# First norm of a two-block network: the input loaded from two queues, root and gain in one operation, 13 warming products

## The chip, the cores and the metric

The kernel runs on one core of a Trainium2 chip. The time is the device time of one execution in microseconds (us); for the kernel before, the median of three runs. Engines: PE is TensorE (matrix products), PEld its weight loads, DVE is VectorE, ACT is ScalarE, POOL is GpSimd, SP is SyncE, which here only issues DMAs. The names with q (SPq, ACTq) are the issue of DMAs on that engine; q1 is SP's DMA queue and q10 ScalarE's.

## The reference

256 positions of width 1024 go through two blocks: the first has two layers (sparse attention and a state-space mixer, each followed by a gated feed-forward), the second one (a gated delta rule with attention to a memory, then a feed-forward). All is float32. The change touches only the first norm and how its input comes in:

```python
def rms_norm(x, gain):
    xf = x.astype(jnp.float32)
    y = xf * lax.rsqrt(jnp.mean(xf * xf, axis=-1, keepdims=True) + RMS_EPS)
    return (y * gain.astype(jnp.float32)).astype(x.dtype)

def first_block(x, norm_gains, nsa_w_in, ...):
    h = x
    for i in range(DEPTH):
        gains = norm_gains[i]
        hn = rms_norm(h, gains[0])
        m = nsa_mixer(hn, nsa_w_in[slot], ...)   # i = 0; its first step is hn @ w_in
...
```

## The kernel before

Each engine has a program of its own, written in order; semaphores join them. Every weight matrix is cut into blocks of 1 MB (128 partitions x 2048 float32), which `sp_load` (L490) fetches into three buffers `raw`, one SP DMA each, in the order of a plan. ScalarE copies a block in two pieces into a high part `whi` (`act_high`, L513), VectorE subtracts to get the low part `wlo` (`dve_low`, L521). The activations are split in the same way into a high and a low `xT`, and TensorE makes every product of three (`pe_three`, L537: low by high, high by low, high by high).

At the start there are two tiles of 128 rows, t = 0 and 1, each in two halves of 512 columns, n = 0 and 1:

- SP issues the four halves of the input into `h` (L2826), then three weight blocks (L496) and small tables. ScalarE issues the identity matrix (L2846, shown as masks<-in_masks) and the gain row, broadcast to 128 partitions, into `grow2` (L617, shown as grow<-in_rows), and loads its activation table.
- ScalarE squares each half with a running sum (`act_norm_sums`, L679). VectorE adds the two sums of a tile (L684), GpSimd takes the power -1/2 (L667).
- Meanwhile VectorE multiplies each half by the gain (`dve_norm_gain`, L697); when the root is there it scales the result in place (`dve_norm_scale`, L704). The halves are then ready in `xs` or `xs1`.
- TensorE starts as soon as the identity has landed with 16 products of it with itself, whose result nobody reads (L3005, the warming products). Then it transposes the halves, four 128x128 pieces each (L725), makes eight more such products (L3009), and begins the first projection with `pe_first` (L1009: first the pieces k 0 to 3 of the high parts, then 4 to 7; then L1015 and L1016 with the low parts).
- ScalarE copies the transposed halves into the high `xT` (L734), tile 0, then a piece of the first weight block (L519), then tile 1, then the next piece; VectorE makes the low `xT` (L741) and low weights (L527) in the same order.

From there on the order around the change is written out by hand; no scheduler decides it. The functions that the change touches follow, with what calls them.

Of the kernel before, what the change touches and what calls it, by code (L numbers as in the profile page):

```python
# [259 lines left out]
def build(nc, wall, x_d, mem_d, cols_d, rows_d, masks_d, neg_d, out_d):  # L260
# [6 lines left out]
    MUL, ADD, SUB = ALU.mult, ALU.add, ALU.subtract  # L267
# [12 lines left out]
    with root:  # L280
# [11 lines left out]
        def up(sem, *event, by=1):  # L292
            return counts[0].up(sem, *event, by=by)

        def at(sem, *event):
            return counts[0].at(sem, *event)
# [4 lines left out]
        def sb(shape, dt=f32, st=root, name="t"):  # L301
            names[0] += 1
            return st.enter_context(nc.sbuf_tensor(f"{name}{names[0]}", shape, dt))
# [16 lines left out]
        h = sb([128, 2, 1024], name="h")  # L320
        xT = [sb([128, 8, 256], f32r, name="xT") for _ in range(2)]
        ss = sb([128, 8], name="ss")
        rr = sb([128, 4], name="rr")
        sqj = sb([128, 1024], name="sqj")
        xs = sb([128, 1024], name="xs")
        grow2 = sb([128, 1024], name="grow2")
# [140 lines left out]
        def rowsrc(name, a=0, n=None):  # L467
            o, w = _ROWS[name]
            n = w if n is None else n
            return rows_d[:, o + a:o + a + n].to_broadcast([128, n])  # L470
# [145 lines left out]
        def act_gain(e, i, name):  # L616
            e.dma_start(gains[i][:, :], rowsrc(name)).then_inc(*up(f"gain{i}", name, by=16))  # L617

        def xs_of(k, t):

            return xs1 if t and k != 4 else xs

        def halves(v):
            return [v[:, 512 * n:512 * n + 512] for n in range(2)]
# [66 lines left out]
        def dve_norm_gain(e, k, t, n, src, gain, ready, turned=None):  # L691

            e.wait_ge(*at("gain1", gain))
            e.wait_ge(*at(*ready[n]))
            if turned:
                e.wait_ge(*at("pe.norm", *turned))
            e.tensor_tensor(halves(xs_of(k, t))[n], halves(src)[n], grow2[:, 512 * n:512 * n + 512], MUL).then_inc(  # L697
                *up("dve.norm", "y", k, t, n))

        def dve_norm_scale(e, k, t):  # L700
            e.wait_ge(*at("pool.norm", "sum", k, t))
            for n, v in enumerate(halves(xs_of(k, t))):
                e.wait_ge(*at("dve.norm", "y", k, t, n))
                e.tensor_scalar(v, v, rr[:, 2 * t + 1:2 * t + 2], None, MUL).then_inc(*up("dve.norm", "xs", k, t, n))  # L704
# [22 lines left out]

        def four(b):
            return b[:, :].rearrange("p (a n) -> p a n", a=4)

        def act_norm_high(e, k, t, ns=range(2)):
            for n in ns:
# [2088 lines left out]


        def sync(e):
            for t in range(2):
                for n in range(2):
                    e.dma_start(h[:, t, 512 * n:512 * n + 512], x_d[128 * t:128 * t + 128, 512 * n:512 * n + 512]).then_inc(  # L2826
                        *up(f"h{t}{n}", by=16))
            for i in range(NRAW):
                sp_load(e, i)
            e.dma_start(cols[:, :], cols_d).then_inc(*up("cols", by=16))  # L2830
            e.dma_start(negf[:, :], neg_d).then_inc(*up("negf", by=16))
            e.dma_start(masks[:, 128:_MASKS], masks_d[:, 128:_MASKS]).then_inc(*up("masks", by=16))
            for o, name in ((0, "dtb"), (32, "alog"), (64, "gdtb"), (72, "galog")):
                e.dma_start(srow[:, o:o + _ROWS[name][1]], rowsrc(name)).then_inc(*up("srow", name, by=16))
            for i in range(NRAW, NCH):
                sp_load(e, i)
            for t in range(2):
                for n in range(2):
                    o = 512 * n
                    e.wait_ge(*at("dve.norm", "h", 5, t, n))  # L2840
                    e.dma_start(out_d[128 * t:128 * t + 128, o:o + 512], h[:, t, o:o + 512]).then_inc(*up("out", by=16))
            e.wait_ge(*last("out"))

        def scalar(e):
            split = Split(lambda p: act_high(e, p), ENDS)
            e.dma_start(ident, masks_d[:, 0:128]).then_inc(*up("ident", by=16))  # L2846
            act_gain(e, 1, "g_nsa")
            e.wait_ge(*at("pool.const", "nhalf"))
            e.activation(rr[:, 0:1], nhalf[:, :], ACTF.Square).then_inc(*up("act.const", "table"))
            for t in range(2):  # L2850
                act_norm_sums(e, 0, t, h[:, t, :], [(f"h{t}{n}",) for n in range(2)])
            act_norm_high(e, 0, 0)
            split.one()
            act_norm_high(e, 0, 1)
            split.to(2)
            act_nsa_in(e, split)
            e.wait_ge(*at("dve.const", "gon"))
            e.wait_ge(*at("srow", "galog"))
            e.wait_ge(*at("dve.norm", "y", 0, 1, 1))
            act_gain(e, 1, "g_ffn0")  # L2860
            walk(NSA_ORDER["act"], {"s": scoring(nothing, lambda n: act_exp(e, n)),
                             "t": turning(nothing, lambda n: act_turned(e, n)),
                             "v": valuing(nothing, lambda t: act_close(e, t), four_steps()),
                             "b": act_nsa_cmp(e), "c": act_nsa_side(e)}, split)
            split.to(C_OUT + 4)
            act_add_norm(e, 0, 1, (C_OUT + 3,))
            split.to(C_OUT + 5)
            act_norm_sums(e, 1, 1, h[:, 1, :], hready(0, 1))
            act_norm_high(e, 1, 1)

            e.wait_ge(*at("dve.norm", "mp", 0, 1, 0))
            act_gain(e, 0, "p_ffn0")
            e.wait_ge(*at("dve.norm", "y", 1, 1, 1))
            act_gain(e, 1, "g_ssd")
            act_ffn(e, split, 0)
            act_boundary(e, split, 1, 2, ffn_done(0), C_S + 2, 2)

            act_ssd_first(e, split)
            e.wait_ge(*at("dve.norm", "mp", 1, 1, 0))
            act_gain(e, 0, "p_ssd")  # L2880
            e.wait_ge(*at("dve.norm", "y", 2, 1, 1))
            act_gain(e, 1, "g_ffn1")
            walk(SSD_ORDER["act"], {"a": scans(lambda g, t: act_seg(e, g, t), lambda g: act_ssd_scan(e, g)),
                             "b": projs(lambda g: act_ssd_proj(e, g), no_steps)}, split)
            split.to(C_SO + 8)
            act_boundary(e, split, 2, 3, [(C_SO + 7, "first"), (C_SO + 7,)], C_SO + 7 + AHEAD, 1)

            e.wait_ge(*at("dve.norm", "mp", 2, 1, 0))
            act_gain(e, 0, "p_ffn1")
            e.wait_ge(*at("dve.norm", "y", 3, 1, 1))  # L2890
            act_gain(e, 1, "g_mem")
            e.wait_ge(*at("pe.norm", 3, 1, 1))
            e.dma_start(memx[:, :, :], mem_d.rearrange("(t p) d -> p t d", p=128)).then_inc(*up("mem", by=16))
            act_ffn(e, split, 1, lambda g: act_mem_rows(e, g))
            act_gdn_in(e, split, ffn_done(1))
            e.wait_ge(*at("dve.norm", "mp", 3, 1, 0))
            act_gain(e, 0, "p_gdn")
            e.wait_ge(*at("dve.norm", "y", 5, 1, 1))
            act_gain(e, 1, "g_ffn2")
            walk(GDN_ORDER["act"], {**{s: chains(i, lambda hp: act_chain(e, hp)) for i, s in enumerate("ab")},  # L2900
                             "c": fill(lambda j: act_gproj(e, j), no_steps),
                             "p": first_pair(lambda j: act_gproj(e, j)),
                             "m": mem_attention(lambda n: act_mem_exp(e, n), lambda n: n % 2 or act_mem_turned(e, n), nothing, lambda: act_mem_end(e))}, split)
            act_boundary(e, split, 4, 6, [(C_GO + 5, "first"), (C_GO + 5,)], C_GO + 5 + AHEAD, 1)

            e.wait_ge(*at("dve.norm", "mp", 4, 1, 0))
            act_gain(e, 0, "p_ffn2")
            act_ffn(e, split, 2)
            for t in range(2):
                act_add_norm(e, 5, t, ffn_done(2)[t])  # L2910

        def vector(e):
            split = Split(lambda p: dve_low(e, p), ENDS)
            e.wait_ge(*at("act.const", "table"))
            for t in range(2):
                for n in range(2):
                    dve_norm_gain(e, 0, t, n, h[:, t, :], "g_nsa", [(f"h{t}{n}",) for n in range(2)])
                dve_norm_sums(e, 0, t)
            for t in range(2):
                dve_norm_scale(e, 0, t)  # L2920
            dve_norm_low(e, 0, 0)
            split.one()
            dve_norm_low(e, 0, 1)
# [76 lines left out]
        def tensor(e):  # L3000
            split = Split(lambda p: None, ENDS)
            e.wait_ge(*at("ident"))

            for _ in range(16):
                e.matmul(banks[0][:, 0:128], ident, ident, start=True, stop=True)  # L3005
            for t in range(2):
                pe_norm_turn(e, 0, t)
# [119 lines left out]
```

## Time and profile before

| | |
|---|---|
| median of 3 runs | 1204.3 us (1203.85 to 1208.6) |
| profiled execution | 1204.32 us |
| its span | 1202.5 us |
| TensorE busy | 1176.9 us, 98% of the span |
| VectorE, ScalarE, GpSimd busy | 70%, 54%, 13% |
| granted TensorE clock | 1.00 in the mean |
| input half, gain row, weight block | 256, 512, 1024 KB per DMA |

The profiled execution agrees with the median. Times in the rows below are counted from the start of the span. A matrix product of two float32 operands of 128x128 (L3005, L3009) is shown as two records of a matmul and two of a weight load, so 16 products are x32. A record's duration is longer than the step from one to the next, since they are pipelined. What stands in square brackets is the idle time before an instruction on its engine, and what ended it; an instruction without a bracket followed the one before at once.

### The profile page before, as it was taken

The numbers are of one execution on the slowest core, as the hardware profiler recorded it, in microseconds if no ns is written. First come the engines' busy times: TensorE is split into PE (matmuls) and PEld (weight loads), VectorE is DVE, ScalarE is ACT, GpSimd is POOL, SyncE is SP. The second block draws the span as 40 slices with busy tenths as digits, with TensorE's granted clock in tenths as the row PEclk, the third lists the DMA queues.
The fourth block names the chain that finished last, engine by engine and source line by source line (L and its number), as shares of the span: only waits on it lengthen the run. The fifth ranks groups of instructions, "written<-read, shape, count | busy, mean of one in ns | idle before, by whom it ended". The sixth has DMA issues, their size and how long they took to land.

```text
span 1202.5 us, 23183 instructions
## 1 busy us (share of the span) xinstructions
PE 1176.9 (98%) x9852; PEld 1076.7 (90%) x9852; DVE 847.2 (70%) x1299; ACT 651.3 (54%) x1171; POOL 151.4 (13%) x143
## 2 busy tenths in 40 slices
PE   8999999999999999999999999999999999999998
PEld 8897789999889898978999988999989878999986
DVE  6677777888557988886788874857577776655542
ACT  4657556666446665644666653665435534644431
POOL 1320000000002332101000000103443311000000
PEclk9999999999999999999999999999999999999999
DMA  8842225565625443353755564442222322755540
GB/s 308 268 141 89 98 101 207 192 210 194 231 106 176 151 182 141 114 184 105 259 196 181 206 245 158 178 176 106 107 107 71 120 93 92 277 196 190 184 167 35
DMA packets 31622, 196.67 MB, mean 164 GB/s; under 512 B 4000, under 2 KB 5664, under 8 KB 9376
## 3 DMA queue, kind: packets, MB, share of 16 engines
q1 hardware_dynamic: 27504, 185.17, 43.1%
q10 hardware_dynamic: 4016, 10.03, 2.6%
q8 instruction: 77, 1.26, 0.5%
q14 instruction: 25, 0.20, 0.0%
HBM read 193.09 MB, written 1.05 MB: 161 GB/s over the span
## 4 chain that ended last, share of the span: by engine, by line
PE 88%; DVE 5%; ACT 3%; issue 2%; POOL 1%; DMA 0%; DVEq 0%; POOLq 0%; ACTq 0%
PE bank L538 24%; PE bank L540 24%; PE bank L539 24%; DVE wlo L527 2%; PE bank L1894 1%; PE bank L1132 1%; PE bank L1189 1%; PE bank L1216 1%; ACT whi L519 1%; PE bank L725 1%; PE bank L2538 1%; PE bank L3005 1%; PE bank L2481 1%; POOL rr L667 0%; PE bank L2525 0%
## 5 line engine op out<-in xcount | busy, mean ns | idle before, releaser
L527 DVE TENSOR_TENSOR wlo<-raw,whi 128x1024 fp32r<-128x1024 f32 x322 | 389.0, 1245 | 87.9 <-ACT whi L519 87.3
L538 PE MATMUL bank<-xT,wlo 128*128 128x256 f32 x1488 | 418.6, 281 | 4.2 <-DVE wlo L527 2.1
L539 PE MATMUL bank<-xT,whi 128*128 128x256 f32 x1488 | 413.1, 278 | 0.0
L540 PE MATMUL bank<-xT,whi 128*128 128x256 f32 x1488 | 413.1, 278 | 0.0
L519 ACT ACTIVATE whi<-raw 128x1024 fp32r<-128x1024 f32 (+1 forms) x349 | 349.2, 1048 | 115.9 <-PE bank L540 86.7
L538 PEld LDWEIGHTS bank<-xT,wlo 128*128 128x128 f32 x1488 | 279.5, 188 | 7.9 <-DVE xc L1601 2.8
L539 PEld LDWEIGHTS bank<-xT,whi 128*128 128x128 f32 x1488 | 279.6, 188 | 0.6 <-issue 0.5
L540 PEld LDWEIGHTS bank<-xT,whi 128*128 128x128 f32 x1488 | 279.4, 188 | 0.0
L667 POOL TENSOR_TENSOR rr<-rr,nhalf 128x1 f32<-128x1 f32 x34 | 24.7, 729 | 710.0 <-DVE rr L655 522.4
L538 PE MATMUL bank<-whi,gT 128*128 128x512 f32 x264 | 104.6, 396 | 0.0
L540 PE MATMUL bank<-whi,gT 128*128 128x512 f32 x264 | 104.4, 395 | 0.0
L539 PE MATMUL bank<-wlo,gT 128*128 128x512 f32 x264 | 104.3, 395 | 0.0
L538 PE MATMUL bank<-whi,xT 128*128 128x256 f32 (+1 forms) x320 | 95.9, 300 | 2.5 <-DVE xT L741 2.5
L539 PE MATMUL bank<-wlo,xT 128*128 128x256 f32 (+1 forms) x320 | 93.0, 291 | 0.0
L540 PE MATMUL bank<-whi,xT 128*128 128x256 f32 (+1 forms) x320 | 93.0, 291 | 0.0
L535 POOL TENSOR_TENSOR wlo<-raw,whi 128x1024 fp32r<-128x1024 f32 x24 | 61.4, 2561 | 118.9 <-ACT whi L519 110.2
L538 PEld LDWEIGHTS bank<-whi,xT 128*128 128x128 f32 x320 | 60.4, 189 | 7.4 <-DVE xT L741 2.8
L539 PEld LDWEIGHTS bank<-wlo,xT 128*128 128x128 f32 x320 | 60.4, 189 | 1.8 <-issue 0.5
L540 PEld LDWEIGHTS bank<-whi,xT 128*128 128x128 f32 x320 | 60.2, 188 | 1.5
L540 PEld LDWEIGHTS bank<-whi,gT 128*128 128x128 f32 x264 | 49.6, 188 | 12.0
L539 PEld LDWEIGHTS bank<-wlo,gT 128*128 128x128 f32 x264 | 49.6, 188 | 11.7
L538 PEld LDWEIGHTS bank<-whi,gT 128*128 128x128 f32 x264 | 49.6, 188 | 11.7
(390 smaller groups left out, 1766.5 us busy)
## 6 DMA issues: line engine op xcount, KB each, us to landing
raw<-in_wall SPq DMA_DIRECT2D x173, 1024.0 KB, 4.8
grow<-in_rows ACTq DMA_DIRECT2D x13, 512.0 KB, 5.3
h<-in_x SPq DMA_DIRECT2D x4, 256.0 KB, 5.3
dsk<-in_rows ACTq DMA_DIRECT2D x4, 256.0 KB, 3.4
memx<-in_mem ACTq DMA_DIRECT2D x1, 1024.0 KB, 10.5
out<-h SPq DMA_DIRECT2D x4, 256.0 KB, 2.0
masks<-in_masks SPq DMA_DIRECT2D x1, 580.0 KB, 13.3
D<-Tx ACTq DMA_DIRECT2D x4, 128.0 KB, 5.8
```

The lines of the kernel that those rows point to most:

```text
L519: e.activation(high, src, ACTF.Copy).then_inc(*up("act.high", p))
L527: e.tensor_tensor(low, src, high, SUB).then_inc(*up("dve.low", p))
L535: e.tensor_tensor(low, src, high, SUB).then_inc(*up("pool.low", p))
L538: e.matmul(out, a[1], b[0], start=start, stop=False)
L539: e.matmul(out, a[0], b[1], start=False, stop=False)
L540: return e.matmul(out, a[0], b[0], start=False, stop=stop)
L667: return e.tensor_tensor(v, v, nhalf[:, :].to_broadcast([128, n]), ALU.pow)
L725: r = e.transpose(tl(turn_bank(k, t, n), j), tl(xs_of(k, t), c), ident)
L1132: r = e.matmul(tl(wbank(2 * m + p), i * (t + 1) + kb), qT[rows, 4 * (g // 2) + h0 + i, 128 * t:128 * t + 128], tl(kz[br][rows, g // 2, :], ...
L1189: r = e.transpose(tl(wbank(n), kb * k + i), tl(aP[place(n)], i * (W // 128) + kb), ident)
L1216: r = e.matmul(banks[6 + g // 2][64 * p:64 * p + 64, 128 * h0:128 * h0 + 128 * k], vv[br][:, kb, 64 * (g + p):64 * (g + p) + 64], aPT[(2 * ...
L1894: r = e.matmul(banks[4][:, 64 * i:64 * i + 64], E[:, i, :], xdt[:, 64 * i:64 * i + 64], start=True, stop=True)
```

## The change

Three things are changed, all in the first microseconds. The halves n = 1 of both input tiles are issued by ScalarE, between the identity and the gain row; SP issues only the halves n = 0 and then goes on to the weights. VectorE no longer multiplies by the gain while it waits for the root: it adds the sums of both tiles, and then one operation per half, `scalar_tensor_tensor`, computes h times root times gain. TensorE makes 13 instead of 16 warming products. ScalarE's wait before it loads the next gain row (L2859) now names the new operation.

```diff
+        def load_h(e, n):
+
+            for t in range(2):
+                e.dma_start(h[:, t, 512 * n:512 * n + 512], x_d[128 * t:128 * t + 128, 512 * n:512 * n + 512]).then_inc(
+                    *up(f"h{t}{n}", by=16))
+
+        def dve_norm_first(e, t):
+
+            e.wait_ge(*at("pool.norm", "sum", 0, t))
+            e.wait_ge(*at("gain1", "g_nsa"))
+            for n in range(2):
+                e.wait_ge(*at(f"h{t}{n}"))
+                e.scalar_tensor_tensor(halves(xs_of(0, t))[n], h[:, t, 512 * n:512 * n + 512], rr[:, 2 * t + 1:2 * t + 2],
+                                       grow2[:, 512 * n:512 * n + 512], MUL, MUL).then_inc(*up("dve.norm", "xs", 0, t, n))
...
         def sync(e):
-            for t in range(2):
-                for n in range(2):
-                    e.dma_start(h[:, t, 512 * n:512 * n + 512], x_d[128 * t:128 * t + 128, 512 * n:512 * n + 512]).then_inc(
-                        *up(f"h{t}{n}", by=16))
+            load_h(e, 0)
...
             e.dma_start(ident, masks_d[:, 0:128]).then_inc(*up("ident", by=16))
+            load_h(e, 1)
             act_gain(e, 1, "g_nsa")
...
-            e.wait_ge(*at("dve.norm", "y", 0, 1, 1))
+            e.wait_ge(*at("dve.norm", "xs", 0, 1, 1))
             act_gain(e, 1, "g_ffn0")
...
             for t in range(2):
-                for n in range(2):
-                    dve_norm_gain(e, 0, t, n, h[:, t, :], "g_nsa", [(f"h{t}{n}",) for n in range(2)])
                 dve_norm_sums(e, 0, t)
             for t in range(2):
-                dve_norm_scale(e, 0, t)
+                dve_norm_first(e, t)
...
-            for _ in range(16):
+            for _ in range(13):
                 e.matmul(banks[0][:, 0:128], ident, ident, start=True, stop=True)
```

How the instructions stand on VectorE from its first one on, before (-) and in the changed kernel (+); `ss` holds the sums, `rr` the roots:

```order
-L697 TENSOR_TENSOR xs<-h,grow 128x512 x2
-L684 TENSOR_SCALAR rr<-ss 128x1
-L697 TENSOR_TENSOR xs<-h,grow 128x512 x2
-L684 TENSOR_SCALAR rr<-ss 128x1
-L704 TENSOR_SCALAR xs<-xs,rr 128x512 x4
-L741 TENSOR_TENSOR xT<-bank,xT 128x4x128 x2
-L527 TENSOR_TENSOR wlo<-raw,whi 128x1024
-L741 TENSOR_TENSOR xT<-bank,xT 128x4x128 x2
+L3072 UNCONDITIONAL_BRANCH
+L684 TENSOR_SCALAR rr<-ss 128x1 x2
+L743 SCALAR_TENSOR_TENSOR xs<-h,rr,grow 128x512 x4
+L756 TENSOR_TENSOR xT<-bank,xT 128x4x128 x2
+L527 TENSOR_TENSOR wlo<-raw,whi 128x1024
+L756 TENSOR_TENSOR xT<-bank,xT 128x4x128 x2
```

Eight operations over the halves have become four, and both sums stand ahead of all of them.

On ScalarE, from its first instruction on (the line numbers move because functions were added):

```order
-L3057 UNCONDITIONAL_BRANCH
-L2846 DMA masks<-in_masks 128x128
+L3068 UNCONDITIONAL_BRANCH
+L2858 DMA masks<-in_masks 128x128
+L734 DMA h<-in_x 128x512 x2
 L617 DMA grow<-in_rows 128x1024
-L2849 ACT_TABLE_LOAD
-L2849 ACTIVATE rr<-nhalf 128x1
+L2862 ACT_TABLE_LOAD
+L2862 ACTIVATE rr<-nhalf 128x1
 L679 ACTIVATE sqj,ss<-h 128x512 x4
```

Two issues of input halves now stand between the identity's and the gain row's, and ahead of the table load.

## Rows read from the trace of the kernel before

**Rows 1.** The page: TensorE's busy time; the chain that ended last, by engine.

```profile
PE 1176.9 (98%) x9852; PEld 1076.7 (90%) x9852; DVE 847.2 (70%) x1299; ACT 651.3 (54%) x1171; POOL 151.4 (13%) x143
...
PE 88%; DVE 5%; ACT 3%; issue 2%; POOL 1%; DMA 0%; DVEq 0%; POOLq 0%; ACTq 0%
```

**Rows 2.** Chain of waits from 0 us: start, duration, what, x records.

```profile
4.22 6.76 PE bank L3005 x32
10.98 1.75 PE bank L725 x16
12.73 1.79 PE bank L3009 x16
```

**Rows 3.** Timeline: start, duration (us), engine, line, operation, [idle before, releaser].

```profile
0.72 1.81 SPq L2826 DMA_DIRECT2D h<-in_x  x4
...
1.17 0.45 ACTq L617 DMA_DIRECT2D grow<-in_rows  x1
...
2.58 1.60 SPq L496 DMA_DIRECT2D raw<-in_wall  x3
...
4.02 0.63 ACT L679 ACTIVATE sqj<-h 128x512 f32<-128x512 f32 x1 [0.87 <-DMA h<-in_x]
...
5.92 0.63 ACT L679 ACTIVATE sqj<-h 128x512 f32<-128x512 f32 x1 [1.18 <-DMA h<-in_x]
...
6.57 1.29 DVE L697 TENSOR_TENSOR xs<-h,grow 128x512 f32<-128x512 f32 x2 [6.57 <-DMA grow<-in_rows]
7.65 0.63 ACT L679 ACTIVATE sqj<-h 128x512 f32<-128x512 f32 x1 [1.00 <-DMA h<-in_x]
...
8.14 0.86 POOL L667 TENSOR_TENSOR rr<-rr,nhalf 128x1 f32<-128x1 f32 x1 [7.32 <-DVE rr L684]
...
8.27 0.62 ACT L679 ACTIVATE sqj<-h 128x512 f32<-128x512 f32 x1
...
9.23 1.82 DVE L704 TENSOR_SCALAR xs<-xs,rr 128x512 f32<-128x512 f32 x4
...
10.82 1.91 PE L725 MATMUL bank<-masks,xs 128*128 128x128 f32 x16
11.45 1.09 ACT L734 ACTIVATE xT<-bank 128x512 fp32r<-128x512 f32 x2 [2.47 <-PE bank L725]
...
12.56 1.95 PE L3009 MATMUL bank<-masks 128*128 128x128 f32 x16
...
14.27 2.40 PE L1009 MATMUL bank<-xT,whi 128*128 128x256 f32 x16
...
15.45 1.01 PEld L1009 LDWEIGHTS bank<-xT,whi 128*128 128x128 f32 x8 [0.20 <-ACT whi L519]
```

**Rows 4.** Line L3005, 4 to 10 and 10 to 13 us: duration ns min/median/max.

```profile
L3005 PE MATMUL bank<-masks x27: 420/422/582, 4.2 to 9.9; 128*128 128x128 f32 x27
...
L3005 PE MATMUL bank<-masks x7: 275/291/422, 9.7 to 10.7; 128*128 128x128 f32 x7
```

**Rows 5.** Timeline of VectorE at 157 us: two three-operand operations.

```profile
157.31 1.41 DVE L664 SCALAR_TENSOR_TENSOR h<-xs,rr,h 128x512 f32<-128x512 f32 x2 [0.73 <-POOL rr L667]
```

**Rows 6.** DMA: queues' packets, MB, share (4.75, 54.75 us); busy by stretch, DMA share, GB/s.

```profile
q10 hardware_dynamic: 16, 0.07, 97.5%
q1 hardware_dynamic: 10, 0.01, 7.9%
...
q1 hardware_dynamic: 9, 0.07, 69.6%
q10 hardware_dynamic: 9, 0.04, 36.0%
...
6.00:7.00 1.00, 1.00 (x7) 1.00 (x6) 0.43 (x1) 0.64 (x2) 0.00 (x0) 1.00 0.87 291
8.00:9.00 1.00, 1.00 (x7) 1.00 (x6) 1.00 (x2) 0.98 (x4) 0.86 (x1) 1.00 1.00 426
```

## What the change is predicted to do

> **What bounds the kernel now.** I read the page's busy shares first [rows 1]: TensorE is busy in 98% of a span of 1202.5 us, and the chain that ended last runs through it for 88%. So a change at the start counts by as much as it moves the moment at which TensorE's dense work begins, no more; after that TensorE is the bound. Second, the chain of waits over the first 16 us [rows 2]: warming products (L3005), transposes (L725), eight more products (L3009). On the chain nothing waits for VectorE or a DMA there: the warming products end after the normalised rows are ready, and they, not the norm, hold the first transpose. Third, the timeline of that stretch [rows 3]: the gain row is used from 6.57, ScalarE's four squares start at 4.02, 5.92, 7.65 (each released by its half of the input) and 8.27 (back to back, so the last half was there), VectorE's last four scalings run from 9.23 to 11.05, TensorE's first transpose starts at 10.82, its first real product (L1009) at 14.27, and its second half waits 0.20 for ScalarE at 15.45. Counting that wait, the dense work starts effectively at 14.27 + 0.20 = 14.47. That is the number to beat.
>
> **Fewer warming products.** 16 products show as 32 records. The granted clock reads 1.00 in all slices, yet 27 records that touch the time before 10.0 last 422 ns and those after it 291 and less [rows 4]: the products go at the pace of the lower level (1.2 GHz) first and of 2.4 GHz from about 10.1, after 5.9 us of unbroken products. From 4.22 to the last slow one at 9.9 there are 26 steps, 0.218 us each. 13 products are 26 records, so the next instruction can start at 4.22 + 26 x 0.218 = 9.9. Against 10.82 this frees 0.9 us, if the rows are ready by then.
>
> **Root and weights in one operation.** VectorE loses four products with the gain and four scalings, which took 1.82 in a row [rows 3], and gets four operations of three operands. Two of that kind take 1.41 together elsewhere, 0.75 for one and 0.66 from start to start [rows 5]. So if the first can start at S, the halves are ready at S + 0.75, S + 1.41, S + 2.07, S + 2.73. The products with the gain used to lie beside the wait for the squares and cost nothing; now the gain row stands directly ahead of the first half. That is the new wait: behind it on VectorE stand all four halves, and TensorE, ScalarE's copies and all else wait for these.
>
> **The loads.** Two halves of the input move from SP's queue to ScalarE's, ahead of the gain. The gain was issued at 1.17; two issues of about 0.45 go before it [rows 3], so now at about 2.07. SP gets to the three weight blocks (1 MB each) two issues earlier, at about 1.65 instead of 2.58: so the first block is now issued before the gain, where it stood 1.4 us behind. The table load and the small square on ScalarE end 0.9 us later, at about 4.05; the squares began at 4.02, so that costs nothing.
> - The input. Without the gain's 0.52 MB ahead of it, at 0.29 MB per us (the rate at 6 to 7 us, rows 6), the last half lands 1.8 us before 8.2, at 6.4. Then the squares run until about 7.2, and with 0.2 on VectorE and 0.86 on GpSimd (the row at 8.14) the roots are done at about 6.9 and 8.3. They are not late.
> - The gain. Where a gain row and a weight block were both under way, nine packets of the one went beside nine of the other in a quarter of a microsecond, 4 KB against 8 KB [rows 6]: they take turns packet by packet, so the block takes two bytes for one of the gain's. Also, before, the input's queue moved next to nothing at 4.75 to 5.0 while the gain filled its own [rows 6], so what is issued earlier holds up what is issued later. Bounds for the landing: with the gain alone behind the input, 0.52 MB at 0.43 MB per us (8 to 9 us, rows 6) is 1.2, so 6.4 + 1.2 = 7.6. With two weight blocks alongside (packets paired off from the start, as the eight packets per DMA engine of each issue would be) it is 2.62 MB, 6.2 us, 12.6. I take one block: 1.57 MB, 3.7 us, so S = 10.1. It is the case nearest to the row at 54.75, where a gain issued shortly behind one block shared the way with that block.
>
> **The sum.** With S = 10.1 the last half is ready at 12.83. Four transposes follow (about 0.11 from start to start, from the 16 between 10.82 and 12.56) with some 0.06 for the signal, then the eight products take 12.56 to 14.27, 1.71. First real product: 12.83 + 0.06 + 0.44 + 1.71 = 15.04. ScalarE is not later than that: its copy of the first turned half came 0.63 after the first transpose, and its last piece before the second half of L1009 4.0 after this (11.45 to 15.45); from a first transpose at 10.91 this gives 15.54, while TensorE asks for it at 15.04 + 0.94. So the 0.20 wait goes, and the start moves from 14.47 to 15.04: 0.6 us later. The profiled execution took 1204.32 for a span of 1202.5, and the median is 1204.3, so the two need no correction: 1204.3 + 0.6 = **1204.9 us**. All in all no change that can be measured: 0.5% (6 us) is what a measurement of this kernel tells from none, and its three runs lie 4.8 apart.
>
> What is costed at nothing: the reload of the weight buffers, which waits for VectorE, shifts with the start, but is needed by TensorE only three blocks (5.6 us of products each) later; the first block arrived before ScalarE came to it at 12.42 without a wait.
>
> On the loads the Trainium skill (DMA: Bandwidth & Descriptors, section "Issuing engines are not separate DMA queues") says that DMAs issued by different engines run on the same 16 DMA engines and that spreading them saves only issue time. The packets taking turns in rows 6 agree with that. It speaks against the first part of the change: by it the input gets ahead only because the gain falls back.
>
> **The rivals.**
> 1. *The gain lands early* (before 9.3). For it: a DMA that is issued earlier holds up later ones, and the gain is issued before two of the three blocks. At S = 7.6 the rows are ready in time, and TensorE goes straight from the warming products at 9.9 into 16 transposes (1.75, plus 0.1 for the slow ones before 10.1), the eight products from 11.75, the first real one at 13.46. ScalarE's chain then gives 9.9 + 0.1 + 0.63 + 4.0 = 14.65 for the second half, against 15.45: 0.8 faster, 1203.5.
> 2. *The input's halves land no earlier than before*, a mechanism of the shared engines: the last at 8.2, its root at 10.14 as before, the gain meanwhile by 9.0. Then the third half starts at 10.2, the last is ready at 11.6, the first real product at 11.6 + 2.2 = 13.8: about 0.6 faster, 1203.7. Against it: the gain's 0.52 MB are no longer between them. The page named above would have it so for the same bytes.
> 3. *The gain lands late*, paired with the second block, at 12.6: every microsecond behind 9.5 is one lost, 17.54 instead of 14.47: 3.1 slower, 1207.4.
> 4. *The clock*, the clearly slower case. The warming products now end at 9.9, and TensorE stands still until S + 0.75, 10.85 by my sum and 13.35 at the late bound. Before, the pace rose at 10.1 after 5.9 us without a gap. If the gap makes it rise only after another 5.9 us, half of that, 2.95, is lost: 1207.9, and with the gain at its late bound 1204.3 + 3.1 + 2.95 = 1210.4. It decides as soon as the gain lands after 9.15. Against it: only 0.2 us of the 5.9 are missing when the products end. The Trainium skill (TensorE: Matmul & The Clock Gate, Part 1) says that the number of slow products at a kernel's start varies between runs of the same kernel; one trace cannot show that.
>
> **How the numbers follow.** Forecast (gain lands between 9.3 and 11.3): 0.42. Rival 1: 0.25. Rival 2: 0.10. Rival 3: 0.15. Rival 4: 0.08. The cases reach from 1203.5 to 1207.9 without the last sum; with 2 us below, because 1200 us of later waits never fall out exactly alike, and 0.6 above, the range is 1201.5 to 1208.5. Faster by over 0.5% (under 1198.3) would need something that no row shows: 0.03. Slower by over 0.5% (over 1210.3) is the far end of rival 4, and what I don't see: 0.06. The same: 0.91.
>
> **What would show it.** Right: the changed timeline has the four squares nearly back to back from about 4 us, VectorE's first three-operand operation released by the gain's DMA near 10, four of them 0.66 apart, TensorE idle before L725, and L1009 (now L1024) first at about 15.0. Rival 1 is seen by L725 following the warming products without a gap, rival 2 by squares released at the old times, rival 3 by a gain at 11.5 or later, rival 4 by transposes and the eight products at 422 ns a record. Wrong as a whole would be a total away from 1204 by more than the first 16 us moved: then something later than the start was touched.

## The result and the profile after

| | before | changed |
|---|---|---|
| median, 20 runs each | 1204.59 us (1203.67 to 1211.88) | 1210.05 us (1208.68 to 1218.07) |
| profiled execution, span | 1204.32, 1202.5 us | 1214.50, 1212.7 us |
| granted TensorE clock, mean | 1.00 | 0.997 |

The changed kernel is slower by 0.45% (ratio 1.0045, 95% interval 1.003 to 1.006), 5.5 us between the medians. The forecast was 1204.9 with a range up to 1208.5: the time lies outside.

First the timeline of the start in the changed kernel (start, duration, engine, line, operation, idle before and releaser). It answers to [rows 3].

```profile
0.72 0.86 SPq L734 DMA_DIRECT2D h<-in_x  x2
...
1.17 0.93 ACTq L734 DMA_DIRECT2D h<-in_x  x2
1.63 1.58 SPq L496 DMA_DIRECT2D raw<-in_wall  x3
2.13 0.45 ACTq L617 DMA_DIRECT2D grow<-in_rows  x1
...
4.02 0.61 ACT L679 ACTIVATE sqj<-h 128x512 f32<-128x512 f32 x1
...
4.12 5.80 PE L3016 MATMUL bank<-masks 128*128 128x128 f32 x26 [4.12 <-DMA masks<-in_masks]
...
5.72 0.63 ACT L679 ACTIVATE sqj<-h 128x512 f32<-128x512 f32 x1 [1.00 <-DMA h<-in_x]
...
9.54 0.63 ACT L679 ACTIVATE sqj<-h 128x512 f32<-128x512 f32 x1 [2.35 <-DMA h<-in_x]
...
13.43 2.74 DVE L743 SCALAR_TENSOR_TENSOR xs<-h,rr,grow 128x512 f32<-128x512 f32 x4 [2.92 <-DMA grow<-in_rows]
...
14.24 3.67 PE L725 MATMUL bank<-masks,xs 128*128 128x128 f32 x16 [4.32 <-DVE xs L743]
...
17.70 3.01 PE L3020 MATMUL bank<-masks 128*128 128x128 f32 x16
...
20.47 2.13 PE L1024 MATMUL bank<-xT,whi 128*128 128x256 f32 x16
```

The warming products end at 9.9, the time that was summed. The last half of the input is squared at 9.54 (before 8.27), the gain row releases VectorE at 13.43 (before 6.57), and TensorE stands still for 4.32 ahead of its first transpose. The first real product starts at 20.47 where it started at 14.27.

TensorE by stretch (busy, records, granted clock, DMA share, GB/s) shows what the pause does:

```profile
12.00:13.00 1.00, 0.00 (x0) 1.00 1.04 434
13.00:14.00 1.00, 0.00 (x0) 0.54 1.02 434
...
16.00:17.00 1.00, 1.00 (x6) 0.50 1.05 430
...
19.00:20.00 1.00, 1.00 (x7) 0.54 0.00 0
20.00:21.00 1.00, 1.00 (x11) 1.00 0.00 0
```

The granted clock falls from 1.00 to 0.50 (2.4 to 1.2 GHz) between 13 and 14 us, after TensorE has done nothing from 9.9 on, and comes back between 19 and 20. All 16 transposes and most of the eight products behind them run at the lower level: the transposes' 421 ns a record (273 before) stand in the next row, which has shortest, median and longest record of line L725.

```profile
L725 PE MATMUL bank<-masks,xs x16: 421/421/473, 14.2 to 17.5; 128*128 128x128 f32 x16
```

Last the DMA queues at 9.5 to 10 us (q1 is SP's, q10 ScalarE's; packets, MB, share of the engines), to be laid beside [rows 6]:

```profile
q1 hardware_dynamic: 19, 0.16, 73.4%
q10 hardware_dynamic: 19, 0.08, 37.8%
```

19 packets against 19. SP's are a weight block's of 8 KB, ScalarE's the gain row's of 4 KB. So the gain gets a third of the bytes.

**Where the rest of the profile differs.** Matching VectorE's operations of both traces, everything from 54 us to 1040 us is later by 5.6 to 6.4 us (5.95 at 54 us, 6.35 at 1040); hardly anything further is lost in 980 us. In the profiled execution the last feed-forward layer then adds 4. That has nothing to do with the change, as the last section shows, and is why the two spans lie 10.2 apart and the medians 5.5.

### The profile page after: what moved, and what is told of

Its sections match the earlier page's. It is cut to its first block, busy times and chain, and to the rows that moved or that the text cites. A ratio compares the mean times of both kernels' runs of the same rounds, so it can differ in the third digit from the quotient of the medians.

```text
span 1212.7 us, 23167 instructions
## 1 busy us (share of the span) xinstructions
PE 1182.6 (98%) x9846; PEld 1082.8 (89%) x9846; DVE 845.4 (70%) x1295; ACT 651.9 (54%) x1171; POOL 149.8 (12%) x143
## 3 DMA queue, kind: packets, MB, share of 16 engines
HBM read 193.09 MB, written 1.05 MB: 160 GB/s over the span
## 4 chain that ended last, share of the span: by engine, by line
PE 87%; DVE 6%; ACT 3%; issue 2%; POOL 1%; DMA 1%; ACTq 0%; DVEq 0%; POOLq 0%
PE bank L538 24%; PE bank L539 24%; PE bank L540 24%; DVE wlo L527 2%; PE bank L1909 1%; PE bank L1147 1%; PE bank L1204 1%; DMA grow<-in_rows 1%; PE bank L1231 1%; ACT whi L519 1%; PE bank L725 1%; PE bank L2553 1%; PE bank L2496 1%; PE bank L2511 1%; PE bank L2507 1%
```

## The experiments

Ratios are to the kernel before, measured beside each. In the second group (gain_on_sp, half_packets, gain_first) that kernel's median was 1208.15, in the first 1204.07 and in the third 1203.88; a time is only compared within its group. The edits shown are against the changed kernel, unless the text says otherwise. Theory A is: a weight block's packets take turns with the gain's and the input's, so both land late; TensorE pauses and its clock halves.

### norm_alone: the loads as before

```diff
 def sync(e):
-            load_h(e, 0)
+            for t in range(2):
+                for n in range(2):
+                    e.dma_start(h[:, t, 512 * n:512 * n + 512], ...)
 def scalar(e):
-            load_h(e, 1)
```

> The changed kernel with the four input halves back on SP's queue as before; one operation per half and 13 warming products stay. Theory A (packets of the weight blocks take turns with the gain row and the last input half, so both land late; TensorE then idles and its clock halves): the gain lands at about 6.6 and the last half at 8.2 as before, the first of the four operations starts at about 9.3 behind both sums, the last half is ready at about 12.0, the first L1009-type product starts at 14.0 to 14.4 against 14.27, total equal to the kernel before within 1 us. Theory B (13 warming products are too few in themselves, or the three-operand form is the cost): TensorE's transposes run at 421 ns a record and the total is 2 us or more above the kernel before.

Measured: 1204.14 against 1204.07 us, ratio 0.9997 (0.9988 to 1.0006). Its timeline:

```profile
4.33 4.53 PE L3018 MATMUL bank<-masks 128*128 128x128 f32 x26 [4.33 <-DMA masks<-in_masks]
...
9.12 2.73 DVE L743 SCALAR_TENSOR_TENSOR xs<-h,rr,grow 128x512 f32<-128x512 f32 x4
...
9.92 2.64 PE L725 MATMUL bank<-masks,xs 128*128 128x128 f32 x16 [1.07 <-DVE xs L743]
...
14.11 2.06 PE L1024 MATMUL bank<-xT,whi 128*128 128x256 f32 x16
```

The first of the four operations starts at 9.12, released by both sums and not by the gain; the first real product at 14.11. TensorE paused for 1.07 and kept its clock. So with the loads as before neither 13 warming products nor the three-operand form costs anything that can be measured: theory B falls, and the loss comes with the loads. The same 26 records of warming products took 4.53 us here, 5.80 in the changed kernel and between 4.70 and 5.86 in the other versions with 13 products, so the moment at which the pace rises differs between executions. That they ended at 9.9 in the changed kernel is partly luck; here they ended at 8.86, and the rows decided.

### loads_alone: only the loads changed

```diff
...
             for t in range(2):
+                for n in range(2):
+                    dve_norm_gain(e, 0, t, n, h[:, t, :], "g_nsa", [(f"h{t}{n}",) for n in range(2)])
                 dve_norm_sums(e, 0, t)
             for t in range(2):
-                dve_norm_first(e, t)
+                dve_norm_scale(e, 0, t)
...
-            for _ in range(13):
+            for _ in range(16):
```

> Only the loads changed: two halves issued by ScalarE ahead of the gain row; the norm (gain product, then scaling) and 16 warming products as before. Theory A: the gain lands at about 13.4, VectorE's four gain products and the second tile's sum run only from there, the last half is ready at about 18, TensorE idles from 10.8 to about 17 and its clock is halved for what follows; first projection product at 21 to 22.5, total 7 to 8 us above the kernel before. Theory B: within 1 us of the kernel before.

Measured: 1212.09 us, ratio 1.0063 (1.0048 to 1.0078), 8.0 us above the kernel before. The timeline:

```profile
13.22 1.29 DVE L697 TENSOR_TENSOR xs<-h,grow 128x512 f32<-128x512 f32 x2 [13.22 <-DMA grow<-in_rows]
...
16.41 3.67 PE L725 MATMUL bank<-masks,xs 128*128 128x128 f32 x16 [6.93 <-DVE xs L704]
...
22.20 2.01 PE L1024 MATMUL bank<-xT,whi 128*128 128x256 f32 x15
```

The gain releases VectorE at 13.22; with the old norm four products and four scalings still follow, and the pause of TensorE is 6.93. From 54 us on the shift is 7.47 us where the changed kernel's is 5.95, so with a late gain the new norm is worth about 1.5 us, because it leaves less to do behind it; when the gain is early it is worth nothing measurable (norm_alone).

### warm31: TensorE kept busy over the gap

```diff
-            for _ in range(13):
+            for _ in range(31):
```

> The changed kernel with 31 instead of 13 warming products, so that TensorE is busy until about 14.2, when the first half is ready. Theory A puts 2 of the 6 us down to the halved clock after the gap: transposes at 273 ns a record, first projection product at about 18.4 instead of 20.5, total 2 us under the changed kernel and some 4 above the one before. Rival (the clock costs nothing there, what is late is only the rows): first projection product at 20.5, total as the changed kernel.

Measured: 1208.28 us, ratio 1.003 (1.0011 to 1.0048), 4.2 above the kernel before. The timeline:

```profile
4.01 9.34 PE L3016 MATMUL bank<-masks 128*128 128x128 f32 x62 [4.01 <-DMA masks<-in_masks]
...
13.31 2.74 DVE L743 SCALAR_TENSOR_TENSOR xs<-h,rr,grow 128x512 f32<-128x512 f32 x4 [2.81 <-DMA grow<-in_rows]
...
14.12 2.64 PE L725 MATMUL bank<-masks,xs 128*128 128x128 f32 x16 [0.77 <-DVE xs L743]
...
18.30 2.13 PE L1024 MATMUL bank<-xT,whi 128*128 128x256 f32 x16
```

The gain is as late as in the changed kernel, the pause only 0.77, and the transposes take 2.64 instead of 3.67. The first real product comes at 18.30 instead of 20.47. Of the 2.17 us between the two, 0.12 are the gain's, which landed at 13.31 and not at 13.43. So 2.05 of the 6 us are the lower clock after the pause, and the remaining 3.95 the late rows. This division is the traces': the medians, each against the kernel before in its own group, lie 4.2 and 5.5 above it, and the intervals of the two ratios overlap.

### weights_wait: no weights beside the gain

```diff
             load_h(e, 0)
+            e.wait_ge(*at("gain1", "g_nsa"))
             for i in range(NRAW):
                 sp_load(e, i)
```

> The changed kernel, but SP issues the first weight block only when the gain row has landed. Theory A: with no weight packets beside it the last input half lands by 6.5 and the gain by 8; TensorE goes from the warming products into the transposes with no gap over 0.5 us at full clock; the first weight block then lands at about 12 and takes the place as the last wait, first projection product at 13.5 to 15.5, total within 1.5 us of the kernel before. Rival C (the gain is late because it is the fourth DMA in ScalarE's own queue, whatever SP moves): the gain lands after 11 here too, and the total is 5 us or more above the kernel before.

Measured: 1211.63 us, ratio 1.0058 (1.0043 to 1.0073). The timeline, and below it TensorE's longest wait up to 80 us (line, releaser, total, times, longest) with its place in the timeline:

```profile
7.39 1.28 SPq L496 DMA_DIRECT2D raw<-in_wall  x3
...
7.75 2.73 DVE L743 SCALAR_TENSOR_TENSOR xs<-h,rr,grow 128x512 f32<-128x512 f32 x4
...
8.54 2.64 PE L725 MATMUL bank<-masks,xs 128*128 128x128 f32 x16
...
14.00 1.15 PE L1024 MATMUL bank<-xT,whi 128*128 128x256 f32 x8 [1.03 <-ACT xT L749]
```

```profile
PE bank L538 <- DVE wlo L527: 5.3, 2, 4.3
...
43.53 0.55 PE L538 MATMUL bank<-xT,wlo 128*128 128x256 f32 x1 [4.28 <-DVE wlo L527]
```

SP's issue of the first block at 7.39 is the moment at which the gain has landed: 7.4 instead of 13.4, from the same fourth place in ScalarE's queue. Rival C falls: the weights beside it made the gain late. The transposes start at 8.54, and the first real product, which now waits for weights, at 14.00. My expected total was wrong all the same, by 6 us: the fourth block reaches ScalarE at 28.17 and not at 22.52 as before, and TensorE waits 5.3 for low parts of weights further on (before 0.9), 4.28 of it up to 43.5. In that pause the granted clock falls to 0.50 and is back only at 48 us, so the pause costs more than its length: VectorE's operations stand 6.6 us later than before from 54 us on. What the first microseconds take from the weights is missing in the next forty.

### gain_on_sp: the gain ahead of the weights, in SP's queue

```diff
 def sync(e):
             load_h(e, 0)
+            act_gain(e, 1, "g_nsa")
 def scalar(e):
             load_h(e, 1)
-            act_gain(e, 1, "g_nsa")
```

> The changed kernel with the gain row moved from ScalarE's queue to SP's, ahead of the first weight block (SP: two halves, gain, weights; ScalarE: identity, two halves). Theory A (packets taking turns): only input and gain are under way together, the last half lands by 7 and the gain by 8.5, the weights no later than in the kernel before; no gap over 0.5 us ahead of the transposes and full clock, first projection product at 13.4 to 13.9 against 14.27, total 0.4 to 0.9 us under the kernel before. Rival D (the weights, a megabyte behind, or a gain issued later than 1.17, cost as much as the norm gains): equal to the kernel before or slower by up to 1 us.

Measured: 1210.48 us against 1208.15, ratio 1.0015 (1.000 to 1.003). Expected was a gain. The timeline:

```profile
10.33 0.63 ACT L679 ACTIVATE sqj<-h 128x512 f32<-128x512 f32 x1 [3.04 <-DMA h<-in_x]
...
11.22 2.73 DVE L743 SCALAR_TENSOR_TENSOR xs<-h,rr,grow 128x512 f32<-128x512 f32 x4
...
12.01 3.67 PE L725 MATMUL bank<-masks,xs 128*128 128x128 f32 x16 [3.01 <-DVE xs L743]
...
18.43 2.13 PE L1024 MATMUL bank<-xT,whi 128*128 128x256 f32 x16
```

Now it is the last half of the input that is late: squared at 10.33, later than in the changed kernel. VectorE's first three-operand operation is no longer released by the gain, but stands behind the second tile's sum, which the new code places ahead of the first tile's halves. TensorE pauses 3.01 and its clock falls here too. Both theories' totals missed: A's was under the kernel before, D's at most 1 us above it. The medians lie 2.3 apart with an interval that reaches down to 0; the traces say it more plainly, the first real product is 3.96 later (18.43 against 14.47) and the spans are 4.0 apart.

Packets taking turns do not explain all of this. By the count of issues the last half (third on ScalarE's queue) stands beside the gain row (third on SP's), and the gain landed at 8.1. The queues from 8 to 9 us:

```profile
q1 hardware_dynamic: 53, 0.43, 102.4%
q10 hardware_dynamic: 8, 0.01, 1.9%
```

ScalarE's queue has next to no bytes left, and yet the half is released only at 10.33, close to the landing of the first weight block (10.6, which is 8.5 after its issue). So there is a tail of about 2 us between the last bytes and the release while the other queue is full of weights. What makes it stays open.

### half_packets: weight blocks in 4 KB packets

```diff
-            e.dma_start(raw[i % NRAW][:, 0:sizes[i]], src).then_inc(*up(f"raw{i % NRAW}", i, by=16))
+            for o in range(0, sizes[i], 1024 if i < NRAW else sizes[i]):
+                w = 1024 if i < NRAW else sizes[i]
+                e.dma_start(raw[i % NRAW][:, o:o + w], src[:, o:o + w]).then_inc(*up(f"raw{i % NRAW}", i, by=16))
```

> The changed kernel with each of the first three weight blocks loaded by two DMAs of 128 rows of 4 KB instead of one of 8 KB; the bytes and their order are the same. Theory A1 (turns packet by packet, whatever their size): against 4 KB packets the last half (2 KB packets) lands at about 7.5 instead of 9.5 and the gain (4 KB packets) at about 10 instead of 13.4, first projection product at about 15 (or 17 if the clock falls in the gap), total 3 to 5 us under the changed kernel. Rival A2 (queues share bytes alike, or simply take their order): the gain still lands at 13 or later, total as the changed kernel.

Measured: 1211.57 us against 1208.15, ratio 1.003 (1.0017 to 1.0044). DMA queues at 8 to 9 us, then the timeline:

```profile
q1 hardware_dynamic: 55, 0.22, 53.7%
q10 hardware_dynamic: 57, 0.22, 52.4%
```

```profile
9.28 0.63 ACT L681 ACTIVATE sqj<-h 128x512 f32<-128x512 f32 x1 [1.58 <-DMA h<-in_x]
...
11.85 2.74 DVE L745 SCALAR_TENSOR_TENSOR xs<-h,rr,grow 128x512 f32<-128x512 f32 x4 [1.60 <-DMA grow<-in_rows]
12.65 3.51 PE L727 MATMUL bank<-masks,xs 128*128 128x128 f32 x16 [2.87 <-DVE xs L745]
...
17.83 2.13 PE L1026 MATMUL bank<-xT,whi 128*128 128x256 f32 x16
```

57 packets against 55, as even as before, but now 0.22 MB each: with packets of one size the two queues share the bytes alike. The gain lands 1.6 earlier, at 11.85, and the first real product is 2.6 earlier than in the changed kernel. The other 1.0 is the clock's: it fell here too, but from the first transpose to the first real product it is 5.18 us (12.65 to 17.83), against 6.23 in the changed kernel and 4.18 in warm31. Rival A2 falls; A1 has the direction and not the size (10 was expected for the gain, and 7.5 for the last half, which came at 9.28, only 0.3 earlier). At 8 to 9 us ScalarE's queue moves 4 KB packets, which are the gain's, so the last half's own rows were out by about then: here too more than a microsecond lies between them and the release.

### gain_first: the gain ahead of the two halves on ScalarE's queue

```diff
-            load_h(e, 1)
             act_gain(e, 1, "g_nsa")
+            load_h(e, 1)
```

> The changed kernel with the gain row issued ahead of the two halves on ScalarE's queue (as early as before, at 1.17). Theory A: the gain lands at about 6.5, but the last half now travels beside weight packets and lands at 9.5 to 11; its root is there 2 to 3 us later, so the second tile's halves are ready at 13 to 14.5, first projection product at 15 to 17, total 1 to 3 us above the kernel before. Rival: the halves are hidden behind the first tile's work, total within 0.5 us of the kernel before.

Measured: 1214.56 us against 1208.15, ratio 1.0047 (1.0029 to 1.0066). The timeline, then the DMA queues at 7 to 8 us:

```profile
10.36 0.63 ACT L679 ACTIVATE sqj<-h 128x512 f32<-128x512 f32 x1 [5.60 <-DMA h<-in_x]
...
13.52 0.63 ACT L679 ACTIVATE sqj<-h 128x512 f32<-128x512 f32 x1 [1.68 <-DMA h<-in_x]
...
15.20 3.68 PE L725 MATMUL bank<-masks,xs 128*128 128x128 f32 x16 [5.12 <-DVE xs L743]
...
21.08 2.13 PE L1024 MATMUL bank<-xT,whi 128*128 128x256 f32 x16
```

```profile
q1 hardware_dynamic: 43, 0.35, 83.7%
q10 hardware_dynamic: 43, 0.09, 22.6%
```

43 packets against 43, 8 KB against 2 KB: the two halves of the input get a fifth of the bytes, and land at 10.36 and 13.5. The first real product starts at 21.08, and the loss is 6.4 us, worse than the 1 to 3 expected, because both halves and not only the last one were caught. Whatever stands last in ScalarE's queue is late; the order there only chooses which.

### masks_late_norm and masks_late_before: the weight stream gets its place back

The first of the two has the input's loads as before besides (norm_alone with this edit), the second is the kernel before with this edit alone.

```diff
-            e.dma_start(masks[:, 128:_MASKS], masks_d[:, 128:_MASKS]).then_inc(*up("masks", by=16))
...
             for i in range(NRAW, NCH):
                 sp_load(e, i)
+                if i == NRAW:
+                    e.dma_start(masks[:, 128:_MASKS], masks_d[:, 128:_MASKS]).then_inc(*up("masks", by=16))
```

> The version with only the new norm and 13 warming products (loads as before), and the large table of masks (580 KB) issued behind the fourth weight block instead of ahead of it. There the new norm began the dense work 0.36 us earlier and gave it back at 39 us, where TensorE waited 0.82 for a weight piece whose block had landed at 23.6 behind that table. Theory A (the weight stream holds back what the start gains): the block lands by 22.5, that wait falls to under 0.3, total 0.3 to 1.2 us under the kernel before. Rival: the block is needed later than it lands anyway, and the total stays equal to the kernel before within 0.2 us.

> The kernel before with the same move of the table alone. Theory A: the earlier landing of the fourth block (22.5 before, about 21 now) removes what TensorE waits for weight pieces before 54 us (0.9 in one wait), total 0 to 0.9 us under the kernel before. Rival: equal within 0.2 us.

norm_alone started its real products 0.36 earlier than the kernel before and ended no earlier: at 39.0 TensorE waited 0.82 for a weight piece. With the table behind the fourth block, in masks_late_norm, ScalarE gets this block at 21.36 instead of 23.60:

```profile
21.36 2.01 ACT L519 ACTIVATE whi<-raw 128x1024 fp32r<-128x1024 f32 x2 [2.96 <-DMA raw<-in_wall]
```

No wait of TensorE for weight pieces is left before 60 us, and from 54 us to 112 us all of VectorE's work stands 0.58 us earlier than in the kernel before. Measured: 1203.82 against 1203.88 us, ratio 1.0000 (0.9992 to 1.0009); with the table moved in the kernel before, 1204.93, ratio 1.0006 (0.9995 to 1.0018). The 0.58 us that the trace shows don't come out in the medians. For masks_late_norm the rival's "equal" fits; the median of masks_late_before lies 1.05 above, outside both forecasts but not clear of its interval.

Nor can the 0.58 be called the new norm's. The trace of masks_late_before, with the old norm, stands 0.46 earlier at 54 us, and its first real product starts 0.26 earlier (14.01), though nothing in its norm was changed. The wait that I wanted to remove there was misread: it lies at 68.0 in the kernel before, behind 54 us, and is still there (0.88 at 67.6). And norm_alone's fourth block came at 23.60 where the kernel before, with the table in the same place, has 22.52; so that the table costs the start its 0.36 is not shown. No version beats the kernel before by more than a measurement can tell.

## Why the prediction was wrong

**Bound, warming products, new norm: right.** The start of the real products is what counts; their delay of 6.0 (20.47 against the effective 14.47) is the shift found at every later point, within 0.4. 13 products ended at 9.9 (in norm_alone, where the pace rose sooner, at 8.86), the four operations took 2.74 (2.73 was summed), and the path behind them holds: with the gain at 13.31 and full clock the sum gives 13.31 + 4.94 = 18.25, and warm31 has 18.30.

**The gain's landing: the term that failed.** "I take one block ... so S = 10.1" should have been 13.4. Of the 5.4 us between the start that was summed (15.04) and the measured one (20.47), 3.3 are this term and 2.05 the clock, for which the sum had nothing. The rule that packets take turns was read rightly from [rows 6], and half_packets and gain_first confirm it. But I took the number of blocks from the likeness to one later place, where a gain followed one block, and not from the count that I had made for the late bound: eight packets per DMA engine and issue on either queue, so that ScalarE's fourth issue meets SP's fourth, the second block. In the changed kernel this block landed at 12.6 (10.5 after its issue), 0.8 ahead of the gain, and the first block at 8.8 (7.2 after its issue), 0.7 ahead of the last half. Even that bound, 12.6, was 0.8 short: from 12.0 to 12.5 us ScalarE's queue moves its last 0.01 MB, and the release comes at 13.43. Such a tail has no term in my sum. The same count gives the last half beside the first block. "The last half lands ... at 6.4" took only the gain away from ahead of it and put nothing in its place; it was 9.54. That the input comes first while the gain falls back was thus half true: the last half of the input fell back too.

**The break-even: right.** Every microsecond behind 9.5 was to be one lost; 13.43 gives 3.9, and 3.95 remain when the clock's share is taken out of the 6.0.

**The clock: dismissed.** Rival 4 named the mechanism and the point from which it decides (a gain later than 9.15), and I gave it 0.08 because the products would end when the clock had nearly risen. The argument was about the rise; what happened is a fall, in the pause. By warm31 it costs 2.05; half_packets, with a pause of 2.87, paid 1.0 (5.18 against 4.18), so the price is no constant. It was also not a separate case: a late gain brings the pause with it, so rivals 3 and 4 should have been one case. Rival 4 even names the sum of both, 1210.4, and I left it out of the range. With the parts measured it is 1204.3 + 3.95 + 2.05 = 1210.3, against 1210.05. That the two sums agree is partly luck, for rival 4 had 3.1 for the gain and 2.95 for the clock, and for a rise that comes late.

**The rule of the Trainium skill** that DMAs issued by several engines share the same 16 DMA engines (DMA: Bandwidth & Descriptors, "Issuing engines are not separate DMA queues"): the traces agree, and it was a warning that I used too little. A second queue brought no rate here (426 GB/s at 8 to 9 us before, 434 at 12 to 13 in the changed kernel); it brought another order, in which the wanted 4 KB and 2 KB packets stand against 8 KB ones. The same page (section "Queues, rings and completion order") says that an engine takes turns between queues packet by packet. By it the packet size decides the share, if the packets it means are those that the profile counts; 9 against 9, 19 against 19, 43 against 43 and 57 against 55 agree.

## What to carry to other kernels

Before an urgent load is moved to another queue, count the packets per DMA engine in both queues: in the changed kernel, half_packets and gain_first it landed no earlier than what had the same place in the other queue, and large packets there took the larger share. That count is a lower bound: with weights in the other queue, about 2 us more went by before the release in gain_on_sp. What held here is the order of the kernel before and of norm_alone, where everything that the start waits for stands, by this count, ahead of the first block. Holding the bulk loads back instead (weights_wait) only moved the loss further on.

A pause of TensorE that is made longer than it was should be priced with the clock: pauses of 0.77, 1.03 and 1.07 us kept it at 1.00 here, those of 2.87, 3.01, 4.28, 4.32, 5.12 and 6.93 were all followed by products at 0.50. A gain of half a microsecond in one trace says little here: masks_late_before stands 0.46 us off the kernel before at 54 us with the same norm.

## What else the runs showed

A mode of the last feed-forward layer, independent of the change. Two consecutive steps of its up projection (VectorE's operation that ends a step), before and in the changed kernel:

```profile
1071.55 0.69 DVE L966 TENSOR_TENSOR gT<-pr,gT 128x512 fp32r<-128x512 f32 x1 [0.70 <-ACT gT L937]
...
1082.43 0.69 DVE L966 TENSOR_TENSOR gT<-pr,gT 128x512 fp32r<-128x512 f32 x1 [0.70 <-ACT gT L937]
```

```profile
1079.40 0.69 DVE L981 TENSOR_TENSOR gT<-pr,gT 128x512 fp32r<-128x512 f32 x1 [0.70 <-ACT gT L952]
...
1090.71 0.69 DVE L981 TENSOR_TENSOR gT<-pr,gT 128x512 fp32r<-128x512 f32 x1 [0.70 <-ACT gT L952]
```

10.88 us a step against 11.31, with the same work, the granted clock at 1.00 in both and TensorE without idle time; from 1040 to 1137 us that adds 4.1 us. The changed kernel's profile, half_packets', gain_first's and masks_late_before's have 11.3, the other profiles 10.9. It does not need the change: masks_late_before, which has neither the new loads nor the new norm, is among them, at 1207.46 us. Probably the times of the kernel before show it as well, though its one profile has 10.88: of its 20 runs twelve lie between 1203.7 and 1205.3 and eight from 1207.7 up, and in the second group 22 of 23 lie from 1207.4 up, which is why its median is higher there. What makes TensorE 4% slower there stays open.
